# New row tables for attention, and five edits around the two merges of a two-layer encoder trunk

## The reference

```python
def forgetting_attention(x, w_in, b_f, w_out):      # D = 1024, H = 16, Dh = 64
    proj = jnp.einsum("bsd,de->bse", x, w_in)       # q, k, v, gate, f_logit
    cum = jnp.cumsum(jax.nn.log_sigmoid(f_logit), axis=1).transpose(0, 2, 1)
    q = heads(q) * (Dh ** -0.5)
    for blk in range(S // Q_BLOCK):                 # 16 blocks of 128 queries
        s = jnp.einsum("bhqd,bhkd->bhqk", q[:, :, q0:q1], k[:, :, :q1])
        s = s + cum[:, :, q0:q1, None] - cum[:, :, None, :q1]
        p = jax.nn.softmax(jnp.where(causal, s, -jnp.inf), axis=-1)
        outs.append(jnp.einsum("bhqk,bhkd->bhqd", p, v[:, :, :q1]))
    return jnp.einsum("bse,ed->bsd", o * jax.nn.silu(gate), w_out)

def rglru_block(x, w_in, conv_w, conv_b, w_a, b_a, w_i, b_i, lam, w_out):
    u, gate = jnp.split(jnp.einsum("bsd,de->bse", x, w_in), 2, axis=-1)
    u = conv_b + sum(u_pad[:, tap:tap + S] * conv_w[tap] for tap in range(4))
    r, i = sigmoid(u @ w_a + b_a), sigmoid(u @ w_i + b_i)   # blocks of 256
    log_a = -8.0 * r * jax.nn.softplus(-lam)
    h = scan(exp(log_a), sqrt(-expm1(2 * log_a)) * (i * u))
    return jnp.einsum("bse,ed->bsd", h * jax.nn.silu(gate), w_out)

x = layer_norm(DEEPNORM_ALPHA * x + h, ln_g[layer], ln_b[layer])
```

## Time and profile before

| | us |
|---|---|
| median of the timed runs | 2367.14 |
| profiled run, device time | 2368.27 |
| its span in the trace | 2366.5 |
| PE busy | 2337.6 (99%) |
| DVE busy | 1345.9 (57%) |
| ACT busy | 1108.3 (47%) |
| POOL busy | 618.5 (26%) |

### The profile page before, as it was taken

One profiled execution on the slowest core, in us unless ns is written; L12 is line 12 of the kernel. 1 busy time (PEld: TensorE's weight loads), 2 busy tenths in 40 slices (PEclk: granted clock), 3 DMA queues, 4 the chain that ended last, 5 costly groups with the idle time before them and its releaser, 6 DMA issues. The chain is left out here.

```text
span 2366.5 us, 36441 instructions
## 1 busy us (share of the span) xinstructions
PE 2337.6 (99%) x13373; PEld 2023.0 (85%) x13373; DVE 1345.9 (57%) x2772; ACT 1108.3 (47%) x2060; POOL 618.5 (26%) x718
## 2 busy tenths in 40 slices
PE   9999999999999999999999999999999999999998
PEld 7888889999887999889999899778888888887887
DVE  4221121241014998999989999836535565667733
ACT  3111111221114888888888888812024565657300
POOL 0000000000000465655666556516420000000354
PEclk9999999999999999999999999999999999999999
DMA  6444443342126455565555665385623354448572
GB/s 208 142 124 115 125 116 108 109 138 93 67 84 161 99 121 116 133 144 135 120 116 132 144 138 120 89 264 157 206 93 123 118 165 133 134 136 307 190 241 97
DMA packets 221305, 328.77 MB, mean 139 GB/s; under 512 B 17468, under 2 KB 144764, under 8 KB 215308
## 3 DMA queue, kind: packets, MB, share of 16 engines
q1 hardware_dynamic: 220616, 325.91, 48.5%
q0 software_dynamic: 512, 0.53, 0.1%
HBM read 199.89 MB, written 126.48 MB: 138 GB/s over the span
## 5 line engine op out<-in xcount | busy, mean ns | idle before, releaser
L990 DVE TENSOR_TENSOR at_pl<-at_tps,at_ph 128x512 fp32r<-128x512 f32 (+3 forms) x640 | 371.9, 604 | 14.2 <-ACT at_ph L913 14.1
L913 ACT ACTIVATE at_ph<-at_tps 128x512 fp32r<-128x512 f32 (+3 forms) x640 | 306.4, 535 | 102.6 <-PE at_ops L842 72.0
L380 ACT ACTIVATE pa_stg<-pa_ps 128x512 fp32r<-128x512 f32 (+1 forms) x120 | 71.8, 598 | 575.4 <-PE pa_ps L272 569.4
L822 PE MATMUL at_tps<-ident,at_probs 128*128 128x128 f32 x2176 | 329.7, 274 | 1.6 <-DVE at_pl L990 1.2
L842 PE MATMUL at_ops<-at_ph,at_val 128*128 128x256 f32 (+1 forms) x1152 | 325.9, 303 | 1.7 <-DVE at_pl L990 1.7
L903 ACT ACTIVATE at_probs<-at_probs,at_least 128x128 f32<-128x128 f32 (+15 forms) x256 | 308.8, 1206 | 0.0
L272 PE MATMUL pa_ps<-pa_xh,pa_wh 128*128 128x512 f32 x760 | 298.8, 393 | 0.0
L842 PE MATMUL at_ops<-at_pl,at_val 128*128 128x256 f32 (+1 forms) x1152 | 298.1, 282 | 0.0
L272 PE MATMUL pa_ps<-pa_xh,pa_wl 128*128 128x512 f32 x760 | 297.3, 391 | 0.0
L272 PE MATMUL pa_ps<-pa_xl,pa_wh 128*128 128x512 f32 x760 | 296.9, 391 | 0.0
L822 PEld LDWEIGHTS at_tps<-ident,at_probs 128*128 128x128 f32 x2176 | 254.5, 141 | 34.2 <-DVE at_pl L990 10.9
(11 more groups left out here) (203 smaller groups left out, 4518.3 us busy)
## 6 DMA issues: line engine op xcount, KB each, us to landing
at_q<-q_halves SPq DMA_DIRECT2D x45, 512.0 KB
at_k<-k_halves SPq DMA_DIRECT2D x45, 512.0 KB
q_halves<-pa_stg SPq DMA_DIRECT2D x32, 512.0 KB, 3.7
k_halves<-pa_stg SPq DMA_DIRECT2D x32, 512.0 KB, 3.7
v_halves<-pa_stg SPq DMA_DIRECT2D x32, 512.0 KB, 3.1
y_gated<-re_work SPq DMA_DIRECT2D x32, 512.0 KB, 2.9
at_val<-v_halves SPq DMA_DIRECT2D x15, 1024.0 KB, 17.4
pa_wst<-in_attn_w_in SPq DMA_DIRECT2D x14, 1024.0 KB, 7.1
```

Of the source, the lines that this page charges most:

```text
L380: nc.scalar.activation(out, source(kind, s), func, scale=scale).then_inc(evac_h, 1)
L822: mm = nc.tensor.transpose(tps[c % TB][:, k, :], probs[s % ROWS][:, t0:t0 + P], ident[:, :])
L913: nc.scalar.activation(ph[g % 2][:, j * PB:j * PB + n, i % 2 * P:(i % 2 + 1) * P], tps[c % TB][:, 0:n, :], ACT.Copy).then_inc(high_out, 1)
L990: nc.vector.tensor_tensor(pl[g % 2][at], tps[c % TB][:, 0:n, :], raw(ph[g % 2][at]), ALU.subtract)\
```

## The change

It does six things.

1. `TENSOR_ROWS` and `VECTOR_ROWS` have new strings, with the same counts of letters.
2. The conversions of weight pieces 0 to 3, one behind each of steps 28 to 31 of the last pair, become those of pieces 0 to 2, all behind step 36. Pieces 3 to 7 follow after attention.
3. On SP the four residual loads leave `behind(GROUPS - 5)`, where they stood ahead of the last y stores, and follow the last y piece; y pieces 2 and 3, the gain, the parameter rows, y pieces 4 and 5 and the first strip are ordered anew.
4. In the first merge DVE sums row n+1 (`sum_rows`) ahead of normalizing row n, for the first four rows.
5. In the last recurrence step but one, ACT takes the root behind the second evacuation instead of the first.
6. `beside` is called in the six tail steps of attention only, no longer in the last pass.

```diff
@@ -541,11 +541,11 @@
     GROUPS = 2 * GT
     PAIRS = D // HEAD_DIM // 2
     PB = BANK // P
-    TENSOR_ROWS = ("VTTVTVTSVVVT", "S", "STTVVTVVVVTVTTVVTV", "SV", "STVVVVVVTVSVVVVTVVV", "SVVVVVS", "SVTS",
...
-    VECTOR_ROWS = ("LXLLLL", "XLLL", "XLLLL", "X", "XLX", "XLX", "XLX", "XLX", "XLXLXLL", "XXLXL", "XXLX", "XLXXL",
...
+    TENSOR_ROWS = ("TVTTSVTVV", "SVTVTTV", "SVVTVTVVTVTTVVVT", "SVVT", "SVVTVSV", "SVSVVVV", "SVVVVVSVVVVT",
...
+    VECTOR_ROWS = ("LLLLXL", "XLLLL", "XLL", "XL", "XX", "XLLX", "XXL", "XLX", "XLXLXL", "XLXLX", "XLXLXL",
...
     n_chunks = [(s % QT) // PB + 1 for s in range(STEPS)]
     first = [sum(n_chunks[:s]) for s in range(STEPS)]
     CH = sum(n_chunks)
@@ -946,10 +946,9 @@
             for it in range(1, PAIRS):
                 for s in range(STEPS):
                     step(it, s, True)
-                    if it == PAIRS - 1:
-                        beside(s)
             for s in range(STEPS, STEPS + 3 + TURN_LAG):
                 step(PAIRS - 1, s, False)
+                beside(s)
 
         def vector(dve, beside):
 
@@ -1110,6 +1108,7 @@
     WP = 4
     CP = KC // WP
     KEPT = ST // 2
+    FIRST = 3
     w_v = w_in.rearrange("(c p) f -> p c f", p=P)
     u_v = us.rearrange("(t p) s -> p t s", p=P)
     g_v = gs.rearrange("(t p) s -> p t s", p=P)
@@ -1418,29 +1417,32 @@
                         load_first_weights(c)
                         if c < KC - 1:
                             load_first_y(c)
-                    for m in range(RING):
-                        load_residual(0, m)
 
             at_sync(sp, behind)
             at["stored"](sp, GROUPS - 1)
             load_first_y(KC - 1)
+            for m in range(2):
+                load_residual(0, m)
+            load_y(0, 2)
+            for m in range(2, RING):
+                load_residual(0, m)
             load_gain(0)
-            for j in range(2, 4):
-                load_y(0, j)
             r0 = 0
             for v in (conv_w, conv_b, b_a, b_i, lam):
                 src = v.rearrange("k (t p) -> (k t) p", p=P)
                 sp.dma_start(rows[r0:r0 + src.shape[0], :], src).then_inc(rows_loaded, 16)
                 r0 += src.shape[0]
-            load_strip(0)
-            for j in range(4, 6):
-                load_y(0, j)
+            load_y(0, 3)
             for n in range(ST - RING):
                 store_rows(0, n)
                 if n < KEPT:
                     sp.wait_ge(x_turned, 2 * n + 2)
                 sp.wait_ge(m_stored[n % RING], 16 * (n // RING + 1))
                 load_residual(0, n + RING)
+                if n < 2:
+                    load_y(0, n + 4)
+                if n == 2:
+                    load_strip(0)
                 if n == 5:
                     load_strip(1)
                 if n in (6, 8):
@@ -1731,11 +1733,12 @@
 
             def beside(s):
 
-                if s >= 2 * ST - 4:
-                    weights_high(0, s - 2 * ST + 4)
+                if s == 2 * ST + 4:
+                    for c in range(FIRST):
+                        weights_high(0, c)
 
             at_scalar(act, beside)
-            for c in range(4, KC):
+            for c in range(FIRST, KC):
                 weights_high(0, c)
             for n in range(ST):
                 if n == RING + 1:
@@ -1768,7 +1771,7 @@
                     tap(n + 1)
                 for k, t in enumerate(itertools.chain(*step_tiles(n))):
                     evacuate(t)
-                    if k == 0:
+                    if k == (1 if n == STEPS - 2 else 0):
                         if n:
                             root(n - 1)
                         if n + 1 < STEPS and new_block:
@@ -1799,14 +1802,19 @@
                 nc.vector.tensor_tensor(m_block(r, xl, c), m_block(r, xl_raw, c), raw(m_block(r, xh, c)), ALU.subtract)\
                     .then_inc(m_split, 1)
 
-            def add_rows(r, n):
-
-                m, b = ST * r + n, n % 2
+            def sum_rows(r, n):
+
+                m = ST * r + n
                 dve.wait_ge(r_loaded[n % RING], 16 * (m // RING + 1))
                 dve.wait_ge(m_products, m + 1)
                 row = residual(r, n).rearrange("p (h d) -> p h d", h=DH)
                 nc.vector.scalar_tensor_tensor(out=row, in0=row, scalar=ALPHA, in1=m_psum(r, n)[:, :, :],
                                                op0=ALU.mult, op1=ALU.add).then_inc(summed, 1)
+
+            def row_stats(r, n):
+
+                m, b = ST * r + n, n % 2
+                row = residual(r, n).rearrange("p (h d) -> p h d", h=DH)
                 dve.wait_ge(summed, m + 1)
                 for h in range(DH):
                     nc.vector.bn_stats(stats[:, b, h, :], row[:, h, :]).then_inc(stat, 1)
@@ -1815,6 +1823,10 @@
                 dve.wait_ge(stat, m * (DH + 2) + DH + 1)
                 nc.vector.tensor_scalar(mean_var[:, b, 1:2], mean_var[:, b, 1:2], LN_EPS, None, ALU.add)\
                     .then_inc(stat, 1)
+
+            def add_rows(r, n):
+                sum_rows(r, n)
+                row_stats(r, n)
 
             def norm_rows(r, n):
                 m, b = ST * r + n, n % 2
@@ -1942,14 +1954,22 @@
 
             def beside(s):
 
-                if s >= 2 * ST - 4:
-                    weights_low(0, s - 2 * ST + 4)
+                if s == 2 * ST + 4:
+                    for c in range(FIRST):
+                        weights_low(0, c)
 
             at_vector(dve, beside)
-            for c in range(4, KC):
+            for c in range(FIRST, KC):
                 weights_low(0, c)
             for n in range(ST):
-                add_rows(0, n)
+                if n < RING:
+                    if n == 0:
+                        sum_rows(0, 0)
+                    row_stats(0, n)
+                    if n + 1 < RING:
+                        sum_rows(0, n + 1)
+                else:
+                    add_rows(0, n)
                 if n == RING:
                     dve.wait_ge(par_turned, 1)
                     nc.vector.tensor_copy(par[:, :, :], gps(1, 1)[:, 0:NPAR * KT].rearrange("p (k t) -> p k t", k=NPAR))\
```

More of the change, by code:

```diff
@@ L543, in attend @@
     PB = BANK // P
-    TENSOR_ROWS = ("VTTVTVTSVVVT", "S", "STTVVTVVVVTVTTVVTV", "SV", "STVVVVVVTVSVVVVTVVV", "SVVVVVS", "SVTS",
-                   "STVTS", "STVVSTVSTV", "STSVTTSV", "SVSTTS", "SVVTSVSTVV", "SVSTVSTVVVSV", "STTSSTVVVVTSVT",
-                   "STVSVTSVTVVST", "SVVTSVVVVSS")
-    VECTOR_ROWS = ("LXLLLL", "XLLL", "XLLLL", "X", "XLX", "XLX", "XLX", "XLX", "XLXLXLL", "XXLXL", "XXLX", "XLXXL",
-                   "XLXXLLX", "XLLXLXLXL", "XLXLXLXL", "XXLLXLX")
+    TENSOR_ROWS = ("TVTTSVTVV", "SVTVTTV", "SVVTVTVVTVTTVVVT", "SVVT", "SVVTVSV", "SVSVVVV", "SVVVVVSVVVVT",
+                   "STVSTV", "STVSTSVTV", "SVSTTSVV", "STSVTVSVV", "STTSTVSVVVT", "SVVTSTTSVVTSVV", "SSVVTVSVVST",
+                   "SVTSTSVSTVT", "SVVVSVTSVVS")
+    VECTOR_ROWS = ("LLLLXL", "XLLLL", "XLL", "XL", "XX", "XLLX", "XXL", "XLX", "XLXLXL", "XLXLX", "XLXLXL",
+                   "XLXLXLL", "XLXLXXL", "XLXXLX", "XLXLXLX", "XLXLLXLX")
     n_chunks = [(s % QT) // PB + 1 for s in range(STEPS)]
```

## The result

The changed kernel takes 2388.99 us (median of four runs, 2387.19 to 2391.92), the kernel before on the same chip 2367.85. The ratio is 1.0089, 95% interval 1.0077 to 1.0102: 21 us slower, where 2371 was forecast and the range ended at 2381. The profiled run's span is 2390.1 against 2366.5.

The account below looks back on a forecast made before the run. Attention was taken as bound by PE, with DVE and ACT near their limits and only waits to win. Attention +16.8, first merge −8.2 and last merge −4.7 gave +3.9 us: 2371, range 2361 to 2381.

Parts of the forecast that it names:

- Row 2's turn: Attention, each head: PE waits 1.10 us for ACT's exponential of row 2, behind group 6's last value step.
- row 7's turn: Attention, each head: the turn can start 8.12 us after group 7's last value step; PE has 6.76 of work, waits 1.36.
- row 1's turn: Attention, each head: ACT takes 12.5 us to row 1's exponential, PE's work 12.1; a wait of 0.4.
- The gain of the new tables on DVE: Attention's wide rows: the new order removes 1.1 us a head of DVE-PE handoffs, worth 16.5 us if nothing else were late.
- The first head: Start of attention: filling of the first head taken as 3.8 us, with no change from the new order.
- Rival C: Attention: the clock falls at the new waits, 24 us on top, 2395; chance 0.05.
- The conversions: End of attention: waits around the weight conversions go, −8.6 us (−7 to −9), with nothing lost behind step 36.
- Load order: First merge: last y piece lands 5.8 us earlier; with sums ahead of normalizations, −8.2 us (−5.5 to −8.5).
- Evacuation: Start of the last merge: PE's wait of 3.08 us and 1.65 of slow clock go, −4.7 (−3.5 to −5).
- A: Attention: ACT doesn't bind, −38 us, 2329, or 2346 if only row 2's does; chance 0.15.
- B: First merge: last y piece still late, set by store, landing and load; +10.4 us, 2377.5; chance 0.09.
- the ACT terms: Attention: three waits for ACT, 0.41 + 1.10 + 1.36 = 2.87 us a head instead of 1.18, +25.4 over fifteen heads.

Follow-up runs that it names:

- rest: The changed kernel with the two row tables set back to the old ones, all other edits kept: 2348.35 us, ratio 0.9915 to the kernel before.

## Why the prediction was wrong

**Row 2's turn, row 7's turn, row 1's turn: the first two right.** 1.10 forecast and 1.09 measured, and taken away by moving one exponential on ACT. For row 7, 8.12 forecast from group 7's end to its turn and 8.12 measured, so the 1.36 of wait is there, though it stands in three pieces ahead of rows 4, 5 and 7 and not in one. Row 1's turn has no wait. Instead 0.4 to 0.5 stand before one of row 15's turns, for a bank that DVE frees behind ACT. The size agrees with 0.41, and that is in part luck: the forecast named neither that turn nor that chain.

**The gain of the new tables on DVE: this step failed.** The forecast had "the old tables ask of DVE 0.96 us more than PE's work takes, the new ones 0.06. So this 1.1 us goes". Most of it didn't go. The 1.18 of the old head is made of handoffs of up to 0.25, and the new order still has about 0.7 in such pieces; new rows 8 to 11 alone leave the period at 49.49, and the new rows from 7 on, behind the old start, add 0.60. The count of work over eight rows says whether DVE falls behind over a stretch, and not what each handoff costs when DVE has hardly any idle time: it is busy 18.03 of 18.44 us in the old order and still 17.95 of 18.44 in the fullest stretch of the new (1028.58 to 1047.02). That this is why the handoffs stay is argued and not shown by a run. With the credit the forecast was 2.87 a head, without it 4.05, and the period says 3.7; 15 × (3.72 − 2.87) = 12.8 us is most of the miss of 17 or 18 between the medians. Of the 0.85 a head, 0.7 are the handoffs that stayed and 0.1 is the late turn.

**The first head: this term was missing.** I had taken its filling over unchanged. The new order puts row 0's turn behind three scores instead of five, a wait that the diff's first strings already show, and the clock can fall behind it. It measured 1.9 us in one profile, 2.9 and 5.2 in two of the changed kernel. Rival C had the mechanism (a short wait brings the clock down) but at the place where it did not happen: the fifteen waits of 1.1 inside attention left the clock at 1.00.

**The conversions: right without the tables**, −8.0 against −8.6. The −8.4 of the account of the two spans agrees by luck: the tables alone already take 3.8 off the end of attention in their profile, and moving the conversions gives 4.6 there. Their cost in the tail was put at nothing because ACT idles there; they slow POOL, which the forecast didn't ask about, without a delay at the end that could be shown.

**Load order: right in mechanism, close in size.** −6.6 in one profile and, without a wait, −8.4 in the other, against −8.2 and its range of −5.5 to −8.5. The forecast of a landing at 30.5 us after attention's end was wrong: it comes at 34.3 and 34.8 in the two traces that show it. I had compared 5.8 us of transfer with the old landing as if nothing else in the chain moved. Undone alone, the order costs 4.9 us of landing, near the 5.8, but from a chain that is later than the one before.

**Evacuation: right**, −4.8 against −4.7: 3.2 of it ahead of the last merge's first matmul and 1.6 behind it. The 1.6 is the clock's and not certain: with the tables alone a wait of 3.19 stands at the same place and the clock stays at 1.00.

**The rivals.** A did not happen. B did in part: the piece landed 3.8 us later than forecast, over its 2.3, with a wait of 1.56 but no fall of the clock; in the second profile of the changed kernel there was no wait. What happened is the forecast's own case beyond its end: the range took 2.4 to 3.2 us of waits a head for the ACT terms, and put no uncertainty at all on the 1.1 that DVE was to give back.

## What to carry to other kernels

Here a new order of work took little off the handoffs of an engine that was busy nearly all the time in that stretch. Count such a gain at nothing until a run shows it, and give it both signs in the range. Where one engine's order is fixed in code and another's comes from a table, follow the chain of the fixed one between two events of the tabled one: that gave the first two new waits here to 0.1 us, but not at which turn each stands. Look at the first pass separately: it starts from empty buffers, and its first wait can cost the clock.

## What the runs showed of the hardware

- Behind the same wait of 1.25 us, in the same place, the granted clock over the next 10 us was 0.50, 0.83 or 1.00 in different executions, two of them of the very same kernel. A wait of about 2.0 was followed by 0.50 in the kernel before and by 1.00 in *rest*, and the one of 3.1 to 3.2 ahead of the last merge by 0.50 before and by 1.00 with the tables alone.
- A DVE instruction with two SBUF inputs slows POOL's elementwise instructions from 0.73 us to 1.0 to 1.7, and is itself slowed (1.22 to 1.66 for 128x1024); with one input POOL stays at 0.73.
- The landing of the last y store took 6.8 to 7.6 us in three profiles with the residual loads issued ahead of it, and 3.8 to 6.0 in three with them behind. In one of the latter a delay of 2 us ahead of the store was gone when it landed.
